# Rotation, second attention and convolution steps moved by a block, in a fused two-model kernel on one core

## The reference, cut to what matters

```python
q = rms_norm_2(q...); k = rms_norm_2(k...)
y_attn = window_attention(q, k, v, sink, rel_bias) @ w_attn_out
c = c_val * sigmoid(c_gate)
c = depthwise_conv(c, conv_w, conv_b)            # 31 taps, 512 channels
c = silu(layer_norm_2(c, conv_ln_g, conv_ln_b))
y_conv = c @ w_conv_out
h = h + (g_attn * y_attn + g_conv * y_conv) @ w_o
```

## Time and profile before

| | |
|---|---|
| median of 3 runs | 2344.09 us (2343.52 to 2345.67) |
| the profiled execution's own time | 2341.95 us |
| its span | 2340.1 us |
| TensorE busy | 2260.5 us, 97% |
| VectorE busy | 1655.2 us, 71% |
| ScalarE busy | 1207.3 us, 52% |
| GpSimd busy | 27.9 us, 1% |
| read from HBM | 407.32 MB, 175 GB/s over the span |
| chain that ended last | PE 84%, DVE 9%, ACT 5%, DMA 1%, issue 1%, POOL 1% |

### The profile page before, as it was taken

How to read it: one execution, slowest core, us unless ns; L and a number is a source line. 1 busy time by engine, 2 the same in 40 slices (tenths; PEclk the granted TensorE clock), 3 DMA queues, 4 the chain that set the end, 5 groups by cost and what they waited for, 6 DMA issues and landing times.

```text
span 2340.1 us, 42550 instructions
## 1 busy us (share of the span) xinstructions
PE 2260.5 (97%) x18166; PEld 2122.6 (91%) x18166; DVE 1655.2 (71%) x2455; ACT 1207.3 (52%) x1897; POOL 27.9 (1%) x28
## 2 busy tenths in 40 slices
PE   7999998999999999999999999999999999999999
PEld 7888987998888998899999898899899989889998
DVE  7777468897787647777676667776676666777666
ACT  3745335454564445455445456654555455575453
POOL 0000000000001000000000000100000000010000
PEclk8999999999999999999999999999999999999999
DMA  9444445777645334555555533455555554245554
GB/s 374 159 145 154 146 171 190 241 258 236 224 134 172 136 127 145 174 195 174 180 180 185 185 126 109 153 185 181 188 172 180 182 188 145 93 151 185 183 186 135
DMA packets 115293, 411.15 MB, mean 176 GB/s; under 512 B 12784, under 2 KB 15984, under 8 KB 114976
## 3 DMA queue, kind: packets, MB, share of 16 engines
q1 hardware_dynamic: 114816, 408.05, 51.9%
q10 hardware_dynamic: 288, 0.39, 0.0%
HBM read 407.32 MB, written 1.06 MB: 175 GB/s over the span
## 4 chain that ended last, share of the span: by engine, by line
PE 84%; DVE 9%; ACT 5%; DMA 1%; issue 1%; POOL 1%; SPq 0%; DVEq 0%; ACTq 0%; POOLq 0%
PE bank L196 83%; ACT arena L240 3%; DVE lo L203 2%; DVE arena L211 2%; DVE arena L203 1%; ACT hi L240 1%; PE bank L200 1%; ACT L240 1%; DMA arena<-WA 1%; POOL arena L203 1%; DVE acc L211 1%; DMA raw<-W 0%; DVE arena L214 0%; DVE xT L211 0%; DVE rs_t L217 0%
## 5 line engine op out<-in xcount | busy, mean ns | idle before, releaser
L196 PE MATMUL bank<-h,hi 128*128 128x256 f32 (+1 forms) x6880 | 1277.3, 287 | 0.0
L196 PEld LDWEIGHTS bank<-h,hi 128*128 128x128 f32 x6880 | 1087.2, 194 | 9.8 <-issue 3.4
L240 ACT ACTIVATE hi<-raw 128x1024 fp32r<-128x1024 f32 x664 | 698.4, 1056 | 761.8 <-PE bank L196 718.0
L196 PE MATMUL bank<-h,lo 128*128 128x256 f32 x3504 | 1018.3, 291 | 18.2 <-DVE h L211 15.0
L203 DVE TENSOR_TENSOR lo<-raw,hi 128x1024 fp32r<-128x1024 f32 x664 | 803.7, 1219 | 106.7 <-ACT hi L240 105.5
L196 PEld LDWEIGHTS bank<-h,lo 128*128 128x128 f32 x3504 | 678.2, 194 | 32.9 <-issue 9.9
L196 PE MATMUL bank<-act,hi 128*128 128x512 f32 x1056 | 373.7, 396 | 0.0
L196 PE MATMUL bank<-act,lo 128*128 128x256 f32 x1056 | 300.3, 284 | 0.0
L196 PE MATMUL bank<-arena 64*64 64x64 f32 (+6 forms) x2994 | 224.9, 263 | 20.5 <-DVE arena L203 20.3
L196 PEld LDWEIGHTS bank<-act,hi 128*128 128x128 f32 x1056 | 199.8, 189 | 45.9
L196 PEld LDWEIGHTS bank<-arena 64*64 64x64 f32 (+3 forms) x2994 | 171.4, 146 | 53.1 <-DVE arena L203 23.9
(11 more groups left out here) (145 smaller groups left out, 1946.2 us busy)
## 6 DMA issues: line engine op xcount, KB each, us to landing
raw<-W SPq DMA_DIRECT2D x664, 512.0 KB, 3.4
ada<-WA SPq DMA_DIRECT2D x80, 512.0 KB, 4.2
arena<-WA SPq DMA_DIRECT2D x16, 512.0 KB, 12.2
arena<-scr SPq DMA_DIRECT2D x2, 1024.0 KB, 9.7
xT<-x SPq DMA_DIRECT2D x1, 1024.0 KB, 7.6
arena<-lora SPq DMA_DIRECT2D x2, 512.0 KB, 9.2
arena<-wsT SPq DMA_DIRECT2D x2, 512.0 KB, 10.0
arena<-lnb SPq DMA_DIRECT2D x2, 512.0 KB, 10.3
```

The source lines that it names most:

```text
L196: return self.done(lambda e: e.matmul(out, l, r, start=start, stop=stop, skip_group_check=True))
L240: return self.done(lambda e: e.activation(out, in_, f, scale=scale, **kw))
```

## The change

1. *Modulation*: one more empty step ahead of `sum`, so each group of four columns takes one more block.
2. *Second attention*: its first scores a block later; the first `out` goes behind the second `max`; the end stays.
3. *Convolution*: in the first step of a pair no diagonal is built, so the first TensorE tap comes a block later; the last comes no later than `conv sum`'s step. Behind the second `conv sum` VectorE adds the four tiles up (512, then 256 columns), and `mean` is one matmul instead of four; the squares are added up the same way for `var`. `norm` and `silu` share a step.
4. *Third branch*: `branch1` takes its banks from GEN.
5. *Rotation*: ScalarE makes all four swapped copies and frees the bank; VectorE's cos product and sum are done one item later (for the last, ahead of the blocks of `v`); GpSimd waits for ScalarE.
6. *conv out*: the sum into `merged` goes from GpSimd to VectorE.

```diff
@@ -324,6 +324,7 @@
                 yield
+        yield
         step("sum", i, l, m0, w, 0, n)
@@ -353,11 +354,11 @@
 def att2_steps(l):
-    s = ["next"]
-    for g in range(2):
-        s += [("scores", g), "next", ("max", g), "next", ("exp", g), "next", ("divide", g), "next", "next", ("turn", g),
-              "next", ("out", g), "next"]
-    return s
+    s = ["next", "next"]
+    for p in range(2):
+        s += [("scores", p), "next", ("max", p)] + [("out", 0)] * p
+        s += ["next", ("exp", p), "next", ("divide", p), "next", "next", ("turn", p), "next"]
+    return s + [("out", 1)]
 
@@ -367,15 +368,16 @@
         while j < CV or built or todo:
+            late = pair and j == 0
             if j < CV:
                 s += [("taps", pair, j)]
                 j += 2
             s += [("pe tap", pair, *t) for t in built]
-            built, todo = todo[:3], todo[3:]
+            built, todo = ([], todo) if late else (todo[:3], todo[3:])
             s += [("diag", pair, *t) for t in built]
             s += ["next"]
         s += [("conv sum", pair)]
-    return s + ["next", ("mean",), "next", ("square",), "next", ("var",), "next", ("norm",), "next", ("silu",), "next", ("split",)]
+    return s + ["next", ("mean",), "next", ("square",), "next", ("var",), "next", ("norm",), ("silu",), "next", ("split",)]
 
@@ -1018,16 +1020,12 @@
                         o = take(CONV, ("cmean", l))
-                        pe.wait_ge(v_cv, ("conv sum", l, 2))
-                        for m in range(4):
-                            i = pe.mm(o[:, 0:256], C("ones"), t256(cacc, m), m == 0, m == 3)
-                        i.then_inc(pe_cv, ("cmean", l))
+                        pe.wait_ge(v_cv, ("conv total", l))
+                        pe.mm(o[:, 0:256], C("ones"), t256(cy2, 0), True, True).then_inc(pe_cv, ("cmean", l))
                     elif what == "var":
                         o = take(CONV, ("cvar", l))
-                        pe.wait_ge(a_cv, ("csq", l))
-                        for m in range(4):
-                            i = pe.mm(o[:, 0:256], C("ones"), t256(cy2, m), m == 0, m == 3)
-                        i.then_inc(pe_cv, ("cvar", l))
+                        pe.wait_ge(v_cv, ("csq total", l))
+                        pe.mm(o[:, 0:256], C("ones"), t256(cy2, 0), True, True).then_inc(pe_cv, ("cvar", l))
                 return step
@@ -1135,7 +1133,7 @@
                     l, p = q
-                    pair(WIDE, item, ("w_branch", 1), l, [("c", (2 * p + j) * 128) for j in range(2)],
+                    pair(GEN, item, ("w_branch", 1), l, [("c", (2 * p + j) * 128) for j in range(2)],
                          ys(v_rw, lambda k: ("ys1", l, k // 2), y1h, y1l), 4)
@@ -1589,10 +1587,20 @@
                         v.tt(o, o, ps(("conv", l, pr)), ADD).then_inc(v_cv, ("conv sum", l, pr), frees=("conv", l, pr))
+                        if pr == 2:
+                            v.wait_ge(v_cv, ("conv sum", l, 2))
+                            v.tt(cy2[:, 0:512], cacc[:, 0:512], cacc[:, 512:1024], ADD).then_inc(v_cv, ("conv half", l))
+                            v.wait_ge(v_cv, ("conv half", l))
+                            v.tt(cy2[:, 0:256], cy2[:, 0:256], cy2[:, 256:512], ADD).then_inc(v_cv, ("conv total", l))
                     elif what == "mean":
                         v.wait_ge(pe_cv, ("cmean", l))
                         v.stt(q4(cyc), bc(ps(("cmean", l))[:, 0:256], 1, [128, 4, 256]), -2.0, q4(cacc), MUL, ADD).then_inc(
                             v_cv, ("cmean", l), frees=("cmean", l))
+                    elif what == "square":
+                        v.wait_ge(a_cv, ("csq", l))
+                        v.tt(cy2[:, 0:512], cy2[:, 0:512], cy2[:, 512:1024], ADD).then_inc(v_cv, ("csq half", l))
+                        v.wait_ge(v_cv, ("csq half", l))
+                        v.tt(cy2[:, 0:256], cy2[:, 0:256], cy2[:, 256:512], ADD).then_inc(v_cv, ("csq total", l))
                     elif what == "norm":
@@ -1602,6 +1610,16 @@
                 return step
+
+            def rope(l, p):
+
+                o, s = qk[:, p * 512:(p + 1) * 512], sw[:, (p % 2) * 512:(p % 2 + 1) * 512]
+                v.wait_ge(a_main, ("swap", l, p))
+                v.wait_ge(d_cst, "cst")
+                v.tt(two(o), two(o), bc(C("cos"), 1, [128, 2, 256]), MUL).then_inc(v_main, ("cos", l, p))
+                v.wait_ge(v_main, ("cos", l, p))
+                v.wait_ge(g_main, ("sin", l, p))
+                v.tt(o, o, s, ADD).then_inc(v_main, ("qk", l, p))
 
@@ -1672,6 +1690,8 @@
                 elif what in ("gmlp v", "v"):
+                    if what == "v":
+                        rope(q[0], 3)
                     f.tiles(32)
@@ -1697,15 +1717,8 @@
                     f.tiles(16)
-                    o, s = qk[:, p * 512:(p + 1) * 512], sw[:, (p % 2) * 512:(p % 2 + 1) * 512]
-                    v.wait_ge(a_main, ("swap", l, p))
-                    v.copy(s[64:96, :], ps(item)[96:128, :]).then_inc(v_main)
-                    v.copy(s[96:128, :], ps(item)[64:96, :]).then_inc(v_main, ("swap", l, p), frees=item)
-                    v.wait_ge(d_cst, "cst")
-                    v.tt(two(o), two(o), bc(C("cos"), 1, [128, 2, 256]), MUL).then_inc(v_main, ("cos", l, p))
-                    v.wait_ge(v_main)
-                    v.wait_ge(g_main, ("sin", l, p))
-                    v.tt(o, o, s, ADD).then_inc(v_main, item)
+                    if p:
+                        rope(l, p - 1)
                 elif what == "attention1":
@@ -1895,7 +1908,10 @@
                     v.wait_ge(a_main, ("gate2", l, 4 + p))
-                    v.stt(gc, gc, 1.0, ps(item), ADD, MUL).then_inc(v_main, item, frees=item)
+                    v.stt(gc, gc, 1.0, ps(item), ADD, MUL).then_inc(v_main, ("conv out gated", l, p), frees=item)
+                    mg = merged[:, p * 512:(p + 1) * 512]
+                    v.wait_ge(v_main, ("conv out gated", l, p))
+                    v.tt(mg, mg, gc, ADD).then_inc(v_main, item)
                     for m in (2 * p - 2, 2 * p - 1) if p else ():
@@ -2278,8 +2294,9 @@
                     a.act(o, ps(item), ACT.Copy).then_inc(a_main)
-                    a.act(s[0:32, :], ps(item)[32:64, :], ACT.Copy).then_inc(a_main)
-                    a.act(s[32:64, :], ps(item)[0:32, :], ACT.Copy).then_inc(a_main, ("swap", l, p))
+                    for r in (0, 32, 64, 96):
+                        a.act(s[r:r + 32, :], ps(item)[r ^ 32:(r ^ 32) + 32, :], ACT.Copy).then_inc(
+                            a_main, *([("swap", l, p)] if r == 96 else []), frees=item if r == 96 else None)
                 elif what == "attention1":
@@ -2421,10 +2438,10 @@
                     for m in (2 * p - 2, 2 * p - 1) if p else ():
-                        a.wait_ge(g_main, ("conv out", l, m // 2))
+                        a.wait_ge(v_main, ("conv out", l, m // 2))
                         merge("m2", l, m, mh)
                     for m in (6, 7) if p == 3 else ():
-                        a.wait_ge(g_main, ("conv out", l, 3))
+                        a.wait_ge(v_main, ("conv out", l, 3))
                         merge("m2", l, m, mh)
@@ -2481,11 +2498,11 @@
                     s = sw[:, (p % 2) * 512:(p % 2 + 1) * 512]
-                    g.wait_ge(v_main, ("swap", l, p))
+                    g.wait_ge(a_main, ("swap", l, p))
                     g.tt(two(s), two(s), bc(C("sin"), 1, [128, 2, 256]), MUL).then_inc(g_main, ("sin", l, p))
                 elif what == "attention1":
                     f.chain(("att1", q[0]), att1_steps(q[0]), nothing, True)
-                elif what in ("branch2", "branch1", "attn out", "v2"):
+                elif what in ("branch2", "branch1", "attn out", "conv out", "v2"):
                     f.tiles(8)
@@ -2515,12 +2532,6 @@
                     f.chain(("att2", q[0]), att2_steps(q[0]), nothing)
-                elif what == "conv out":
-                    l, p = q
-                    f.tiles(8)
-                    mg = merged[:, p * 512:(p + 1) * 512]
-                    g.wait_ge(v_main, item)
-                    g.tt(mg, mg, gC[:, p * 512:(p + 1) * 512], ADD).then_inc(g_main, item)
                 elif what == "ple":
                     f.tiles(10)
 

```

## The result

The changed kernel takes **2302.26 us** (median of 4 runs, 2299.89 to 2303.85) against 2343.81 for the kernel before, measured beside it: a ratio of 0.9823 (95% interval 0.9806 to 0.984), 41.5 us less. The forecast was 2307.0 (2298 to 2321), faster. The profiled execution took 2303.23 us, its span is 2301.4; the sum of the prediction gave 2305.1 for such an execution.

A forecast was written before the change was run, and what follows sets the result against it. TensorE, busy 97% of the span, bounds the kernel, mostly waiting for VectorE. Terms 7.2 + 6.0 + 8.3 + 9.2 + 4.5 + 4.2 - 2.5 = 36.9 off 2341.95 give 2305.1; plus 2.1 for the median, 2307 us, range 2298 to 2321.

The forecast's parts named there:

- the first model's rest: Modulation's sums and third branch, net of costs in `wout` and `branch0` 7: 6.0 + 8.3 - 0.8 - 0.5 = 13.0 us gained.
- Rotation, 7.2: `qk` items, both layers: three TensorE stops for the recurrence's mask go, 2 x (0.98 + 0.97 + 1.68) = 7.2 us; bounds 3.6 to 9.7.
- The 1.22 of `v`: TensorE's 1.22 us stop in `v`, claimed to stay because the last rotation still stands in one piece ahead of `v`'s blocks.
- The rule on contention: Rotation: VectorE and GpSimd contend, so each of eight products stretches a split by up to 0.7 us, costing at most 2 us.
- Third branch and sums, 13.0 net: `branch1` 0 stop (6.0) and late sums in `up` and `down` with half clock (8.3), less costs 0.8 and 0.5 us.
- First tap, 9.2: `gate2` 1, each mixer: stop and half clock of 7.1 us go, 2.5 come back; 2 x (7.1 - 2.5) = 9.2, bounds 0 to 14.2.
- Returns whole: Rival: the convolution's stop returns whole behind exp and the diagonals; 2316 us, chance 0.17.
- Statistics, 4.5: Convolution's mean and squares: four matmuls become one, 1.1 us saved each, four times, 4.5 us.
- VectorE's two adds are early by about 0.5 us: Convolution's statistics: adds of 0.7 + 0.4 us fit the block between; if not, they cost up to 1 each.
- The end, 4.2: `conv out` waits for the split go in both layers (2.3), and the bank wait at `wo` (1.9): 4.2 us, bounds 2 to 5.4.
- the banks of `wo` 0: `wo` of layer 0 no longer lands on banks of `conv out` 2 and 3, but on the attention's: 1.9 us gained.
- `c` 0 of layer 1, -1.2: `c` 0 gets bank 1, just filled by the last `f down` matmul; TensorE waits for update and hand-overs, 1.2 us lost.

The follow-up runs named there:

- x1: Changed kernel with the rotation put back: two swapped copies on VectorE, cos product, wait and sum inside the item; 2314.15 us, ratio 0.9883.
- x2: Changed kernel with the modulation's sum again one block behind its last accumulation; 2314.57 us, ratio 0.9887.
- x4: Changed kernel with the order of the convolution's taps and of the second attention's steps as before; 2314.48 us, ratio 0.9886.
- x5: Changed kernel with the convolution's mean and mean of squares as four matmuls each again, without VectorE's four adds; 2306.11 us, ratio 0.9837.
- x7: Changed kernel with a block again between the convolution's normalization and its SiLU; 2302.38 us, ratio 0.9821.
- x6: Changed kernel with the add of the convolution's branch into `merged` on GpSimd again; 2302.5 us, ratio 0.9827.
- x3: Changed kernel with `branch1` on the WIDE banks again, shared with `wout` and `wo`; 2307.46 us, ratio 0.9858.
- x10: Kernel of x9 plus the normalization-SiLU block back and the convolution's bank for `c` 0 of layer 1; 2283.32 us, ratio 0.9748.
- x9: Changed kernel with matmuls of the recurrence's second-chunk steps x and y grouped by row count; leaves out part of the state's products; 2286.9 us, ratio 0.9762.
- x11: Kernel of x10 with start flags only on each bank's (and half's) first matmul, and x's state products of both banks first; 2279.84 us, ratio 0.9734.

## Why the prediction was right, and where it was not

The time came out 4.7 us under the forecast, inside the range. Of that, 1.9 are the terms; 2.1 came from adding the distance of the profiled execution to the median of before; and this time the profiled execution was 1.0 above its median (rounding took 0.2 off). That the terms are off by so little in all is in part luck: rotation, first tap and statistics gave 5.9 more than said, the end and the first model's rest 4.1 less.

- **Rotation, 7.2: held, a little small.** No stop in `qk` 1 to 3, as said. The 1.22 of `v`, which I left standing, went in layer 0 and became 0.88 in layer 1. x1 gives 4.2 a layer. The rule on contention (the Trainium skill, GPSIMD Engine Reference, Specifications) shows in the other direction from the one weighed: the splits did not lengthen (mean 1220 ns, 1219 before), as the products now fall beside none of them, and GpSimd's product got shorter, 1.09 instead of 1.50 to 1.59 us, where VectorE has no cos product beside it any more; the last one of each layer, beside VectorE's cos product, takes 1.60.
- **Third branch and sums, 13.0 net: held (12.4).** `branch1` 0 has no stop and no bank's wait. The sums of `up` 4 and `down` 0 have none, and the gain there is 3.25 of stops and 5.1 of clock, as said. By the page's rule on waits this short (the Trainium skill, TensorE: Matmul & The Clock Gate, HAM oscillation) the clock should not have fallen; in x2 it fell behind 1.55 and not behind 1.76. So the measurements hold against the rule in some executions and not in others, and the term is worth anything from 3.3 to 8.3. Two costs were mis-sized: the wait in `wout` of layer 1 is 1.47 and costs 1.6, not 0.8; the one at `branch0` 7 is 0.86 and 1.7 of half clock behind it, not 0.5.
- **First tap, 9.2: right mechanism, term too small; 11.8 in x4, 12.4 between the traces of before and after.** The loss before was 7.2 a mixer, as said. What comes back, ScalarE's diagonals behind its exps, stands where I put it, two steps after the first tap, but is 1.47 and no clock with it, not 2.5; and the second attention's transposes no longer wait, 0.4 a mixer, which I had left out. "Returns whole" is out.
- **Statistics, 4.5: half right.** TensorE saves 5.2. But the step "VectorE's two adds are early by about 0.5 us" failed: TensorE comes to `conv out` 0 earlier by 2.6 in each layer, the bank that it needs only by 1.3, so 2.6 in all come back there (x5). That the adds are what holds the chain back is likely, but no run shows them apart from the matmuls.
- **The end, 4.2: this is the step that failed; it gave 0.7.** I wrote that `conv out` waits 1.13 for the split, "which now comes a block earlier: 2.3". The split is earlier, but VectorE reaches it before ScalarE has SiLU and rounding done and stands 3.64 us. It stood 3.63 there before too, but then the eviction of `attn out` 1 was done ahead of the wait; now it is behind it, and TensorE waits 1.56 for that bank. I had priced the wait that went and not asked what is queued behind the one that came. Nor does the block fail by itself: with the statistics as before the wait is 0.26 (x5), so it is the two together that turn 1.13 into 1.56. Put back one at a time, the block is worth -1.5 (x7), what the statistics give back is -2.6 (x5), GpSimd's add moved +1.2 (x6), and the banks of `wo` 0 are the +1.9 that I had, with the clock 2.9 (x3). That is 0.0 in all against 0.7 measured; parts that share a wait do not add up exactly.
- **`c` 0 of layer 1, -1.2: held** (0.97 of wait; x10 gets 1.2 back).

## What to carry to other kernels

When a step moves up by a block, look at each in-order engine for what is queued behind its wait, banks to be emptied above all; where the producer isn't ready, the engine waits as long as before (3.63 and 3.64 us) and holds back more. Group matmuls of one row count, and within a group let neighbours write different halves of the partitions: in two steps and two layers this gave some 19 us here (15.4 in x9, 3.5 more in x11), about 8 of it by fewer changes between 64 and 128 rows, about 6 by halves side by side, and the rest, an estimate from these, by the clock. If an accumulation is spread over time in a bank, only the first matmul of that bank and its rows may start it.

## What the runs showed of the hardware

- A change of row count between matmuls costs 0.14 us: 16 fp32 products of 64 columns take 6.14 us alternating between 64 and 128 rows (the last 0.7 of it at half clock) and 3.53 in two groups. In y 7.59 became 3.04 with the same 48 records, and more than half of that is another thing: products of 128 rows that write the lower and the upper 64 partitions in turn pass at one record in 0.06 us, others at one in 0.11 to 0.12. The Trainium skill (TensorEngine Tiling (Array Packing), Key Properties) states that a change of tiling mode drains TensorE; the traces agree in that each change costs time.
- The granted clock fell to half (1.2 GHz) with TensorE busy throughout: 14.27 us busy of 14.27 at 0.64. With no wait ahead of it, it fell only in x, alternating or in four groups (x9); in the one trace of x11, where x is two groups, it did not fall once from `qk` to `wout` of either layer. Why x lowers it stays open.
- Behind waits of 0.86 to 2.56 us it fell in some executions and places and not in others: behind 0.86 in the changed kernel and not in x11, behind 1.55 and not 1.76 in x2, behind 2.56 in layer 0 of x1 and not behind the same wait in layer 1. Costs of the clock behind such a wait are to be given as a range from nothing up.
